# Attention on one core: the first head's transposed probabilities copied by VectorE ahead of its maxima, the fifth chunk of both heads by ScalarE

## The reference, cut to what matters

```python
def sink_attend(q, k_parts, v_parts, masks, sink_g):
    scale = ATT_HD ** -0.5
    logits = []
    for kp, m in zip(k_parts, masks):
        s = jnp.einsum('bqkgd,bskd->bkgqs', q, kp).astype(F32) * scale
        if m is not None:
            s = jnp.where(m, s, -jnp.inf)
        logits.append(s)
    ...
    p = jax.nn.softmax(jnp.concatenate(logits + [sink_col], axis=-1), axis=-1)
    ...
    for vp in v_parts:
        n = vp.shape[1]
        term = jnp.einsum('bkgqs,bskd->bqkgd', p[..., off:off + n].astype(vp.dtype), vp)
        out = term if out is None else out + term
        off += n
```

## Time and profile before

| | us |
|---|---|
| median of 3 runs | 3780.85 |
| lowest and highest run | 3780.5, 3790.98 |
| the profiled execution's own time | 3782.25 |
| its span in the trace | 3780.5 |
| TensorE busy | 3038.9 (80% of the span) |
| VectorE busy | 1219.4 (32%) |
| ScalarE busy | 673.1 (18%) |
| GpSimd busy | 330.8 (9%) |
| mean granted TensorE clock | 0.911 of full speed |

### The profile page before, as it was taken

The page is one execution under the profiler, slowest core; times in us unless marked ns, Lnnn a source line. Parts: engine busy times, 40 slices in busy tenths (PEclk is TensorE's granted clock), DMA queues, the critical chain, the costliest instruction groups (busy, mean ns, idle before and its releaser), DMA issues. The chain is left out here.

```text
span 3780.5 us, 50933 instructions
## 1 busy us (share of the span) xinstructions
PE 3038.9 (80%) x18238; PEld 1582.7 (42%) x18239; DVE 1219.4 (32%) x2221; ACT 673.1 (18%) x1516; POOL 330.8 (9%) x366
## 2 busy tenths in 40 slices
PE   3999999799976947999998457758889659969992
PEld 1455454588852433333333133335554323323330
DVE  3313413576664351111110342126663421101114
ACT  2212111111130100000000121136661100000002
POOL 0000000211110000000000302111110000000002
PEclk9999999899988968999999768879999779989996
DMA  6511110232334436788988320031101359886874
GB/s 259 159 42 55 35 37 28 79 102 69 97 135 175 172 146 256 319 314 359 389 309 352 139 104 24 29 123 41 62 21 41 145 194 406 354 371 274 364 319 161
DMA packets 152814, 667.46 MB, mean 177 GB/s; under 512 B 26128, under 2 KB 62128, under 8 KB 121936
## 3 DMA queue, kind: packets, MB, share of 16 engines
q1 hardware_dynamic: 123568, 540.05, 37.3%
q0 software_dynamic: 19504, 72.03, 5.0%
q10 hardware_dynamic: 9584, 53.19, 3.4%
HBM read 595.84 MB, written 69.39 MB: 176 GB/s over the span
## 5 line engine op out<-in xcount | busy, mean ns | idle before, releaser
L1795 PE MATMUL bank<-w,xT 128*64 (+1 forms) x3392 | 752.5, 601 | 54.0 <-DMA w<-in_moe_w 43.0
L498 PE MATMUL bank<-aT,w 128*128 128x512 f32 (+1 forms) x1344 | 496.5, 532 | 6.7 <-DVE short L680 5.9
L1795 PEld LDWEIGHTS bank<-w,xT 128*64 128x64 f32 x3392 | 244.4, 139 | 522.7 <-issue 514.0
L1815 PE MATMUL bank<-w,hT 128*64 (+1 forms) x1696 | 381.1, 602 | 37.9 <-issue 37.7
L498 PEld LDWEIGHTS bank<-aT,w 128*128 128x128 f32 x1344 | 263.6, 197 | 235.0 <-issue 219.9
L1887 DVE TENSOR_TENSOR h<-h,bank 128x512 f32<-128x512 f32 x53 | 36.4, 687 | 785.0 <-PE bank L1795 785.0
L1815 PEld LDWEIGHTS bank<-w,hT 128*64 128x64 f32 x1696 | 124.8, 138 | 292.6 <-issue 290.4
L2081 PE MATMUL bank<-at_w_in,aT 128*128 128x512 f32 x416 | 191.5, 622 | 2.9 <-PEq L116 2.9
L2269 PE MATMUL bank<-eye,probs 128*128 128x128 f32 x640 | 98.8, 286 | 45.7 <-ACT probsT L2333 45.5
L1771 PE MATMUL bank<-eye,x 128*128 128x128 f32 x440 | 65.5, 295 | 82.6 <-DMA x<-moe_x,idx_block 58.1
L2081 PEld LDWEIGHTS bank<-at_w_in,aT 128*128 128x128 f32 x416 | 83.2, 203 | 105.6 <-issue 105.6
(11 more groups left out here) (333 smaller groups left out, 3918.7 us busy)
## 6 DMA issues: line engine op xcount, KB each, us to landing
w<-in_moe_w SPq DMA_DIRECT2D x180, 2048.0 KB, 14.2
ada_w<-in_ada_w SPq DMA_DIRECT2D x48, 1024.0 KB, 7.9
moe_y<-y ACTq DMA_DIRECT2D x53, 512.0 KB
w<-in_moe_w ACTq DMA_DIRECT2D x12, 2048.0 KB, 27.5
w<-in_ab_w_in SPq DMA_DIRECT2D x28, 512.0 KB, 3.9
moe_y<-zero POOLq DMA_DIRECT2D x1, 8192.0 KB, 27.6
moe_x<-a SPq DMA_DIRECT2D x13, 512.0 KB, 2.6
at_w_in<-in_at_w_in SPq DMA_DIRECT2D x3, 2048.0 KB
```

The source lines that it names most:

```text
L498: mm = pe.matmul(k.bank[3 * s + n][:, 0:width], w[j][:, c, :], aT[:, c, at:at + width], start=(c == 0), stop=(c == KC - 1))
L1795: mm = pe.matmul(k.bank[UP[half]][u * UNIT:(u + 1) * UNIT, :], xT[:, c, u * UNIT:(u + 1) * UNIT], w13[:, r if u else ds(buf[0], 1), half, ...
L1815: mm = pe.matmul(k.bank[Y[half]][u * UNIT:(u + 1) * UNIT, :], hT[:, c, u * UNIT:(u + 1) * UNIT], w2[:, r if u else ds(buf[0], 1), at:at + ...
```

## The change

The two kinds of copy change hands. VectorE copies head 0's four chunks (512 columns), and does so after `divide(m)` and ahead of `maxima(m+2)`. ScalarE copies head 1's four chunks as before, then the fifth chunk of both heads (256 columns). The waits of TensorE on the two turning banks follow the new owners. No instruction is added in sum, nothing else moves.

```diff
@@ wait_fill
-        elif x % 3 == 2:
+        elif x % 3 == 0:
             pe.wait_ge(pt_dve, primed(2 * g + x // 3 + 1))
         else:
-            pe.wait_ge(pt_act, primed(4 * g + 2 * (x // 3) + x % 3 + 1))
+            pe.wait_ge(pt_act, primed(4 * g + 2 * (x // 3) + x % 3))
@@ scalar
-            for h in R2:
-                act.wait_ge(turned, primed(3 * m + h + 1))
-                if m % 2 == 0 and h == 0 and g >= 2:
-                    act.wait_ge(o_ready, primed(g - 1))
-                nc.scalar.copy(pt[g % 2][:, 0:4, h, m % 2, :],
-                               k.bank[6 + fill(m, h) % 2][:].rearrange("p (c n) -> p c n", c=4)).then_inc(pt_act, 1)
+            act.wait_ge(turned, primed(3 * m + 2))
+            if m % 2 == 0 and g >= 2:
+                act.wait_ge(o_ready, primed(g - 1))
+            nc.scalar.copy(pt[g % 2][:, 0:4, 1, m % 2, :],
+                           k.bank[6 + fill(m, 1) % 2][:].rearrange("p (c n) -> p c n", c=4)).then_inc(pt_act, 1)
+            act.wait_ge(turned, primed(3 * m + 3))
+            nc.scalar.copy(pt[g % 2][:, 4, :, m % 2, :],
+                           k.bank[6 + fill(m, 2) % 2][:, 0:2 * P].rearrange("p (h n) -> p h n", h=2)).then_inc(pt_act, 1)
@@ vector
             divide(m)
+            dve.wait_ge(turned, primed(3 * m + 1))
+            if m % 2 == 0 and g >= 2:
+                dve.wait_ge(o_ready, primed(g - 1))
+            V.tensor_copy(pt[g % 2][:, 0:4, 0, m % 2, :],
+                          k.bank[6 + fill(m, 0) % 2][:].rearrange("p (c n) -> p c n", c=4)).then_inc(pt_dve, 1)
             if m + 2 < M:
                 maxima(m + 2)
-            dve.wait_ge(turned, primed(3 * m + 3))
-            if m % 2 == 0 and g >= 2:
-                dve.wait_ge(o_ready, primed(g - 1))
-            V.tensor_copy(pt[g % 2][:, 4, :, m % 2, :],
-                          k.bank[6 + fill(m, 2) % 2][:, 0:2 * P].rearrange("p (h n) -> p h n", h=2)).then_inc(pt_dve, 1)
```

## The result

The change makes the kernel slower: 3817.48 us (median of 4 runs, 3814.01 to 3817.92) against 3780.68, a ratio of 1.0096 with a 95% interval of 1.0074 to 1.0118. That is 36.8 us, about 1%. The forecast was 3801 with a range up to 3810: the sign was right, the size was not.

The account below looks back on a forecast made before the run. A loop of waits among TensorE, ScalarE and VectorE bounds attention, no engine being full. 30 x (1.19 - 0.55 = 0.64) = 19.2, plus 1.1 for the first group, gave +20.3 us: median 3801, range 3789 to 3810.

Parts of the forecast that it names:

- The loop and its parts: Attention's loop of waits between engines: four parts make 10.13 us a group before, 10.77 after the change.
- The copy ahead of the even maxima: VectorE, even steps: head 0's copy delays the next maxima by 1.19 us a group, bounds +1.06 to +1.27.
- The shorter tail: From ScalarE's exponentials to the output products: 0.55 us shorter a group, bounds -0.48 to -0.60.
- The work costed at nothing: Odd maxima, ScalarE's even copies, even fifth chunk's turn, GpSimd's diagonal, `att` and DMA issue: no added time.
- The first group: Attention's first group: its later copy, plus 0.61, less 0.55, adds 1.1 us.
- the clock as a rival: TensorE in attention falls to 1.2 GHz in some groups; one in four gives 35 us more, 3836; chance 0.04.
- the term of the delay and the tail: Attention's groups: 30 steps at +0.64 us each add 19.2 us.
- Rival 1 (faster): Attention's copies run side by side, even maxima not held: 31 x -0.55 = -17 us, 3764; chance 0.05.

Follow-up runs that it names:

- the run with even steps alone: The change kept in even steps only, odd steps as in the kernel before: 3847.55 us, ratio 1.0171.
- the run with odd steps alone: The change kept in odd steps only, even steps as in the kernel before: 3762.05 us, ratio 0.9945.
- The repeats: Odd-step transposes repeated in TensorE's wait: on the change, fifth chunk five times 3795.28 us, twice 3798.67; on the change in even steps only, head 1 four times 3819.04.
- the two traces of the change: The changed kernel, traced once in each of two sets with no edit between: 3817.48 us, then 3809.44 us.
- the fastest version: Even steps as in the kernel before; in odd steps VectorE copies both heads ahead of its maxima, ScalarE the fifth chunk: 3757.06 us, ratio 0.9934.
- the copy behind the even maxima: The change, but in even steps VectorE's copy of head 0 stands behind its maxima: 3832.49 us, ratio 1.0131.

## Why the prediction was wrong in size

- *The loop and its parts.* Right. The full-clock group is 10.71 us against 10.77 forecast.
- *The copy ahead of the even maxima, +1.19.* Right: 1.19 by the run with even steps alone, and the copy's step is the 0.61 taken. The 0.69 that the prediction took from the Trainium skill's sentence on the drain ("VectorE: DVE Perf Modes", "The DRAIN you can't avoid") did not come: the maxima started 0.08 before the copy's recorded end. The same section adds that a next operation that isn't held starts earlier, and with that the trace agrees.
- *The shorter tail, -0.55.* Nearly right: -0.61 by the run with odd steps alone, 0.01 past its bound of -0.60. In the changed kernel the output starts 1.11 behind the exponentials, 0.56 sooner (2703.24 against 2702.13); the other 0.05 come in the output itself, whose first twelve products take 1.47 in place of 1.52.
- *The work costed at nothing.* Right for the odd maxima, GpSimd's diagonal and `att`: ScalarE's odd exponentials again follow the inverse row at once.
- *The first group, +1.1.* Measured +0.8.
- **The step that failed: the clock as a rival at 0.04, with nothing in the sum.** I argued that "the longest idle hardly grows, from 1.23 to about 1.2 plus a 0.6 ahead of it, with work between". Measured were 1.30, and 0.56 ahead of it with 0.44 of work between. The longest wait indeed did not grow (1.29 or 1.30 already stood in every fourth group before), but it was the wrong thing to go by: I took two waits so close together for nothing new, though the earlier trace rows had a stretch of equal busy share at 0.81. The clock fell in 8 of 30 groups. The 30 groups last 334.56 us (from the first `att` to the 31st), and 30 x 10.71 is 321.3: 13.3 us over, 1.66 for each long group. The repeats show the cause: the same program with work in the wait has no such group.
- *The rival's own numbers.* "One group in four", 8 groups, is what came, but nothing in the prediction derived it: that match is luck. I had priced one such group at 4.4, by half speed over TensorE's whole part of the loop; the clock came back at about 2717.9, as the scores of the next step began, so the price was under half of it.
- The sum as measured: before, the 30 groups last 304.55 us, 10.15 on the mean (7 are 10.20 or 10.21), so the term of the delay and the tail is 321.3 - 304.55 = 16.75 where I had 19.2; with 13.3 for the clock and 0.8 for the first group it makes 30.8 us. The spans of the two traces of the change are 35.0 and 23.5 above that of before, the medians of the two sets 36.8 and 27.9. In the traces, what is over or under lies in stages that the change doesn't touch; for the medians that is not shown.
- *Rival 1 (faster)* was wrong for the whole: the maxima are held, by 1.19. Its price, the tail's gain alone, is what the odd steps alone have (3762 measured, 3764 worked out), since nothing there holds the even maxima.

## What to carry to other kernels

Ask of every copy that is handed to another engine what stands behind it in that engine's order, separately for each parity of a loop: here the same edit cost 1.19 us in even steps and gained 0.61 in odd ones, and doing only the good half, then more of it, made 3757 us out of 3780. Where a change adds idle time to TensorE's loop, compare all its waits and not the longest alone, and price the matmuls behind them at the low clock for a part of the passes, even if the stage stood at 1.00 before. A few repeated transposes in a wait are a cheap way to test whether the clock is at work, but shorter waits are better: the fastest version needed no repeats.

## What the runs showed of the hardware that I had not expected

- At waits of 0.24 and 1.23 us a group, or 0.24 and 1.30 as in every fourth, no group lost the clock. With waits of 0.35, 0.56 and 1.30, every third or fourth did, in a pattern that two traces repeat (8 of 30 both times). With 0.22 us more work, none.
- In the change the clock is still at 1.00 in the wait and at 0.50 in the work that follows, from 0.8 to 1.1 us behind the wait's end: the wait's own rows look harmless, and the cost shows as slower matmuls (10.12 us busy in place of 8.49). With the copy behind the even maxima the low clock began some 0.2 us before the end of a wait in 7 of 21 cases, and behind one in the others.
- Repeated transposes were enough to keep the clock full: in the three kernels that have them in the wait, all 90 groups stood at 1.00.
- The start of attention moved between 2509.0 and 2526.8 us over the ten traces of kernels that are identical up to there, so totals of this program can differ by 10 us and more that no edit made.
